# A gated projection from rounded parts and rests, and 20 of 31 depthwise taps as stacked diagonals in four column groups

## The reference, cut to what matters

```python
def conformer_conv_mixer(x, w_in, b_in, dw_w, dw_b, ln_g, ln_b, w_out, b_out):
    a = x @ w_in + b_in
    u = a[..., :D_MODEL] * jax.nn.sigmoid(a[..., D_MODEL:])
    u = causal_dwconv(u, dw_w, dw_b)
    u = jax.nn.silu(layernorm(u, ln_g, ln_b))
    return u @ w_out + b_out
```

## Time and profile before

| | us |
|---|---|
| three runs | 3436.68, 3441.87, 3441.95 (median 3441.87) |
| the profiled execution, first to last instruction (span) | 3435.1 |
| PE busy | 3336.9 (97%) |
| DVE busy | 2003.6 (58%) |
| ACT busy | 1111.1 (32%) |
| POOL busy | 134.1 (4%) |
| mean granted clock of PE | 0.989 |

### The profile page before, as it was taken

How to read it: one execution, slowest core, us unless ns; L and a number is a source line. 1 busy time by engine, 2 the same in 40 slices (tenths; PEclk the granted TensorE clock), 3 DMA queues, 4 the chain that set the end, 5 groups by cost and what they waited for, 6 DMA issues and landing times. The chain is left out here.

```text
span 3435.1 us, 38647 instructions
## 1 busy us (share of the span) xinstructions
PE 3336.9 (97%) x13840; PEld 2509.0 (73%) x13840; DVE 2003.6 (58%) x2815; ACT 1111.1 (32%) x1503; POOL 134.1 (4%) x230
## 2 busy tenths in 40 slices
PE   6999899998999999999999999999999999999999
PEld 3446788886678888667888854588887757888887
DVE  6684666535668864565766359766644464455523
ACT  2223422223632222444433210343333343242222
POOL 1000000000000000000000040000000100000000
PEclk9999999999999999999999999999999999999999
DMA  7222355542125543212223311122233222222222
GB/s 287 80 70 80 131 181 192 176 133 74 49 86 199 192 147 104 68 44 80 94 95 95 96 58 56 51 86 98 96 95 129 79 74 74 98 92 86 97 98 86
DMA packets 100426, 361.20 MB, mean 105 GB/s; under 512 B 11152, under 2 KB 11168, under 8 KB 100064
## 3 DMA queue, kind: packets, MB, share of 16 engines
q1 hardware_dynamic: 79088, 280.34, 24.6%
q0 software_dynamic: 20080, 75.27, 6.6%
q10 hardware_dynamic: 1152, 4.19, 0.3%
HBM read 357.66 MB, written 2.10 MB: 105 GB/s over the span
## 5 line engine op out<-in xcount | busy, mean ns | idle before, releaser
L2393 DVE TENSOR_TENSOR weight_lo<-weight_ring,weight_hi 128x1024 fp32r<-128x1024 f32 (+1 forms) x458 | 552.9, 1208 | 899.2 <-ACT weight_hi L1654 893.3
L1654 ACT ACTIVATE weight_hi<-weight_ring 128x1024 fp32r<-128x1024 f32 (+1 forms) x458 | 478.7, 1046 | 1558.8 <-PE proj_banks L919 972.3
L919 PE MATMUL proj_banks<-h_lo,weight_hi 128*128 128x512 f32 x1672 | 650.5, 389 | 0.0
L919 PE MATMUL proj_banks<-h_hi,weight_hi 128*128 128x512 f32 x1312 | 510.5, 389 | 0.5 <-DVE weight_lo L2393 0.5
L919 PE MATMUL proj_banks<-h_hi,weight_lo 128*128 128x512 f32 x1312 | 510.4, 389 | 0.0
L919 PEld LDWEIGHTS proj_banks<-h_lo,weight_hi 128*128 128x128 f32 x1672 | 313.8, 188 | 64.9
L919 PEld LDWEIGHTS proj_banks<-h_hi,weight_hi 128*128 128x128 f32 x1312 | 246.3, 188 | 52.3 <-issue 0.8
L919 PEld LDWEIGHTS proj_banks<-h_hi,weight_lo 128*128 128x128 f32 x1312 | 246.3, 188 | 51.0
L919 PE MATMUL proj_banks<-mid_lo,weight_hi 128*128 128x512 f32 x704 | 273.9, 389 | 0.0
L919 PE MATMUL proj_banks<-mid_hi,weight_lo 128*128 128x512 f32 x704 | 273.9, 389 | 0.0
L919 PE MATMUL proj_banks<-mid_hi,weight_hi 128*128 128x512 f32 x704 | 273.9, 389 | 0.0
(11 more groups left out here) (426 smaller groups left out, 5200.2 us busy)
## 6 DMA issues: line engine op xcount, KB each, us to landing
weight_ring<-in_w_up SPq DMA_DIRECT2D x176, 512.0 KB, 3.3
ada_ring<-in_ada POOLq DMA_DIRECT2D x96, 512.0 KB, 3.8
weight_ring<-in_w_dn SPq DMA_DIRECT2D x64, 512.0 KB, 3.5
weight_ring<-in_w_br SPq DMA_DIRECT2D x32, 512.0 KB, 3.2
weight_ring<-in_w_upr SPq DMA_DIRECT2D x32, 512.0 KB, 3.2
weight_ring<-in_w_dnr SPq DMA_DIRECT2D x32, 512.0 KB, 3.2
weight_ring<-in_w_dn SPq DMA_DIRECT2D x32, 384.0 KB, 3.1
cond<-in_ada POOLq DMA_DIRECT2D x20, 512.0 KB, 4.6
```

The costliest lines, as they stand in the source:

```text
L919: last = mm(proj.banks[:, u % RING, :], stationary(home + n)[:, w], moving(k), start=k + m == 0, stop=k == kt - 1 and m == 2)
L1654: return nc.scalar.activation(out, in_, func, **kw)
L2393: return v.tensor_tensor(out, a, b, op)
```

## The change

The projection `ca` joins `SPLIT`: weights and normed activations are split into rounded parts and rests, `first_three` does its tiles 0 to 2 (the third tile's weights go to a free part of the scratch memory), the other 13 are done by `split_feature_tile`. ACT and DVE split two chunks for each channel tile, placed between their other work. SP's loads for `ca` are written out instead of looped.

DVE keeps 11 taps of each channel tile; PE does 20. For these, SP copies `u` inside the SBUF: for each of the four groups of 32 channels, four copies, each one token further along, go to the four groups of 32 partitions (`spread_rows`, 16 DMAs of 32 x 528 floats for each tile, with two buffers in turn). One matmul then has 128 rows, four taps of 32 channels, and 32 columns: a 128 x 32 matrix in which four 32 x 32 diagonals are stacked (`stacked`). Five such matmuls, each four tokens further, make the 20 taps of 32 channels, and the four channel groups write the four groups of 32 partitions of one bank (`depthwise`). GpSimd makes all 20 x 4 small diagonals of a tile by one product of 128 x 640. The taps of tile t stand after the `ca` tile 2t + 3; those of the last tile stand between the sums of the first four tiles and of the last four.

```diff
+TAP_GROUPS = 5
+OWN_TAPS = CONV - 4 * TAP_GROUPS
+SPREAD = S + 4 * (TAP_GROUPS - 1)
...
+    def spread_rows(t):
+
+        if t >= 2:
+            sp.wait_ge(*c.mix.filled(("dw", t - 2)))
+        sp.wait_ge(*proj.emptied(("ca", 2 * t)))
+        u = c.T(0, 9)[:, t * PAD:(t + 1) * PAD]
+        for q in range(4):
+            for shift in range(4):
+                sp.dma_start(spread_taps(c, t)[32 * shift:32 * shift + 32, q, :],
+                             u[32 * q:32 * q + 32, OWN_TAPS + shift:OWN_TAPS + shift + SPREAD]).then_inc(s[f"taps_spread{t % 2}"], 16)
...
             load(name, n, first + n)
+            if name == "ca" and n >= 5 and n % 2 == 1:
+                spread_rows((n - 5) // 2)
+            if name == "cout" and n % 2 == 1:
+                spread_rows(6 + n // 2)
...
+    taps = 4 * TAP_GROUPS
     for t in range(KD):
-        for n, k in enumerate(range(CONV - PE_TAPS[t], CONV)):
-            nc.gpsimd.tensor_scalar(diagonal(c, t, n), c.square("ident"), c.v("c_dw_w_2", 8 * k + t), None, ALU.mult) \
-                .then_inc(s["diag_ready"], 1)
+        out = c.T(30, 10)[:, t * taps * 32:(t + 1) * taps * 32].rearrange("p (n i) -> p n i", i=32)
+        nc.gpsimd.tensor_tensor(out, c.const("eye32").unsqueeze(1).broadcast_to([P, taps, 32]),
+                                c.v("c_dw_stacked", t * taps, taps).unsqueeze(2).broadcast_to([P, taps, 32]), ALU.mult) \
+            .then_inc(s["diag_ready"], 1)
...
-    for t in range(KD + 1):
-        if t == 0:
-            feature_tile("ca", 0, H, ready=h_ready(6))
-            feature_tile("ca", 1, H)
-            continue
-        if t < KD:
-            feature_tile("ca", 2 * t, H)
-        if t == KD:
-            sum_squares(("lnm", 0), lambda k: (s["u_ready"], k + 1), lambda k: T(11 + k), KD, end=2)
-        pe.wait_ge(*proj.emptied(("ca", 2 * t - 2)))
-        pe.wait_ge(s["diag_ready"], TAPS_BEFORE[t])
-        u = T(0, 9)[:, (t - 1) * PAD:t * PAD]
-        bank = open_bank(mix, ("dw", t - 1))
-        for n, k in enumerate(range(CONV - PE_TAPS[t - 1], CONV)):
-            last = mm(bank, diagonal(c, t - 1, n), u[:, k:k + S], start=n == 0, stop=k == CONV - 1)
+    def depthwise(t):
+
+        pe.wait_ge(s["diag_ready"], t + 1)
+        pe.wait_ge(s[f"taps_spread{t % 2}"], 256 * (t // 2 + 1))
+        bank, x = open_bank(mix, ("dw", t)), spread_taps(c, t)
+        for g in range(TAP_GROUPS):
+            for q in range(4):
+                last = mm(bank[32 * q:32 * q + 32, :], stacked(c, t, g, q), x[:, q, 4 * g:4 * g + S], start=g == 0, stop=g == TAP_GROUPS - 1,
+                          skip_group_check=True)
         last.then_inc(mix.full_sem, 1)
-        if t < KD:
-            feature_tile("ca", 2 * t + 1, H)
-    sum_squares(("lnm", 0), lambda k: (s["u_ready"], k + 1), lambda k: T(11 + k), KD, first=2)
+
+    u_tile = lambda k: T(11 + k)
+    u_ready = lambda k: (s["u_ready"], k + 1)
+    first_three("ca", 6, c.H_lo)
+    for t in range(3, 16):
+        split_feature_tile("ca", t, c.H_hi, c.H_lo)
+        if t % 2 == 1:
+            depthwise((t - 3) // 2)
+    sum_squares(("lnm", 0), u_ready, u_tile, KD, end=4)
+    depthwise(7)
+    sum_squares(("lnm", 0), u_ready, u_tile, KD, first=4)
...
         copy_out(proj, ("ca", 2 * t + 1), T(9 + t % 2), ACT.Sigmoid, bias=c.v("c_b_in_2", 8 + t))
+        for n in range(2 * t + 3, min(2 * t + 5, 16)):
+            round_chunk("ca", n)
...
+    def add_spread(t):
+
+        dve.wait_ge(*mix.filled(("dw", t)))
+        st.last(tt(T(11 + t), T(11 + t), mix.bank(("dw", t)), ALU.add), mix.emptied(("dw", t)))
+        dve.sem_inc(s["u_ready"], 1)
+
     for t in range(KD):
-        u = u_all[:, t * pad:(t + 1) * pad]
-        if t < KD - 1:
-            gated(t)
-        acc, own = T(11 + t), CONV - PE_TAPS[t]
+        u, acc = u_all[:, t * pad:(t + 1) * pad], T(11 + t)
+        gated(t)
+        if 2 * t + 3 < 16:
+            rest_chunk("ca", 2 * t + 3)
         st.link(ts(acc, u[:, 0:S], c.v("c_dw_w_2", t), ALU.mult, c.v("c_dw_b_2", t), ALU.add))
...
+        for k in range(1, OWN_TAPS):
             st.link(stt(acc, u[:, k:k + S], c.v("c_dw_w_2", 8 * k + t), acc, ALU.mult, ALU.add))
...
+        if t >= 1:
+            add_spread(t - 1)
+        if 2 * t + 4 < 16:
+            rest_chunk("ca", 2 * t + 4)
+    add_spread(7)
```

More of the change, by code:

```diff
@@ L107, in other_constants @@
         "pick_wide": np.tile(np.eye(4, 32).reshape(1, 128), (P, 1)),
+        "eye32": np.tile(np.eye(32), (4, 1)),
     }
@@ L143 @@
     ("norm_mix_2", 2 * D), ("norm_ffn_2", 2 * D), ("norm_final_2", D), ("m_conv_w_2", 4 * D), ("m_conv_b_2", D),
-    ("m_head_norm_2", D), ("c_b_in_2", 2 * D), ("c_dw_w_2", CONV * D), ("c_dw_b_2", D), ("c_ln_g_2", D),
+    ("m_head_norm_2", D), ("c_b_in_2", 2 * D), ("c_dw_w_2", OWN_TAPS * D), ("c_dw_stacked", 4 * TAP_GROUPS * D), ("c_dw_b_2", D), ("c_ln_g_2", D),
     ("c_ln_b_2", D), ("c_b_out_2", D), ("f_conv_w_2", 2 * 3 * 2 * FF), ("f_conv_b_2", 2 * 2 * FF),
@@ L171 @@
 STAGE = {s[0]: s for s in STAGES}
-SPLIT = ("abo", "up0", "dn0", "sq", "sk", "sv", "cu", "cdo", "up1", "dn1", "mqk", "mv", "mo", "mout", "up2", "dn2", "cout", "up3", "dn3", "rk", "rq", "rv", "fv", "ru", "rg", "br", "ro", "upr", "dnr")
-SPLIT_NORMS = (1, 2, 3, 4, 5, 7, 9)
+SPLIT = ("abo", "up0", "dn0", "sq", "sk", "sv", "cu", "cdo", "up1", "dn1", "mqk", "mv", "mo", "mout", "up2", "dn2", "ca", "cout", "up3", "dn3", "rk", "rq", "rv", "fv", "ru", "rg", "br", "ro", "upr", "dnr")
+SPLIT_NORMS = (1, 2, 3, 4, 5, 6, 7, 9)
 def pieces(k_tiles):
@@ L389, in __init__ @@
             "gla_hi", "gla_lo", "dsa_hi", "pool_hi", "sb_hi", "m_hi", "m_lo_ready", "u_hi", "u_lo", "merged_hi", "merged_lo", "pooled", "z_ready", "k_scaled", "sp_ready", "lw_ready", "w_ready", "wneg_ready",
-            "diag_ready", "convolved", "conv_init", "conv_act", "mid_raw", "mid_rounded", "mid_ready", "w_rounded", "w_split", "third_rounded", "third_split", "w_used", "h_raw", "h_rounded", "m_gate", "m_rows", "m_guard", "e_arg", "e_ready",
+            "diag_ready", "taps_spread0", "taps_spread1", "convolved", "conv_init", "conv_act", "mid_raw", "mid_rounded", "mid_ready", "w_rounded", "w_split", "third_rounded", "third_split", "w_used", "h_raw", "h_rounded", "m_gate", "m_rows", "m_guard", "e_arg", "e_ready",
             "p_head", "hm_ready", "hsq_ready", "den_abs", "u_ready", "u_centred", "u_sq", "u_normed", "u_act",
@@ L596, in hi @@
             at = self.third[n][0]
-            return self.mid_hi[:, at * S:(at + 2) * S]
+            return (self.relu_r if n == self.first_split["ca"] + 2 else self.mid_hi)[:, at * S:(at + 2) * S]
         return self.w_hi[:, (n % SPLIT_RING) * SLOT:(n % SPLIT_RING + 1) * SLOT]
@@ L603, in lo @@
             at = self.third[n][1]
-            return self.mid_lo[:, at * S:(at + 2) * S]
+            return (self.relu_r if n == self.first_split["ca"] + 2 else self.mid_lo)[:, at * S:(at + 2) * S]
         return self.w_lo[:, (n % SPLIT_RING) * SLOT:(n % SPLIT_RING + 1) * SLOT]
@@ L667 @@
 PLAIN = {4: ("norm_mix_2", 0), 5: ("norm_ffn_2", 0), 6: ("norm_mix_2", 8), 7: ("norm_ffn_2", 8)}
-PLAIN_SPLIT = (4, 5, 7)
+PLAIN_SPLIT = (4, 5, 6, 7)
 SQ0, RSTD = 44, 54
@@ L714, in sync_program @@
             continue
-        looped = kind in ("loop", "branch")
+        looped = kind in ("loop", "branch") and name != "ca"
         for n in range(RING if looped else total):
@@ L1686, in round_third @@
         name = SPLIT_UP[r]
-        if NORM_AFTER[r] in ("dn0", "dn1"):
+        if NORM_AFTER[r] in ("dn0", "dn1", "dn2"):
             act.wait_ge(*split_use(c, c.first_split[NORM_AFTER[r]] + 3 * (KD - 1)))
@@ L2331, in scalar_program @@
         root_token("dnr", t, c.late_tile(4 + t))
-THIRD = {1: (16, 20), 2: (0, 2), 3: (16, 20), 4: (6, 0), 5: (14, 20), 7: (20, 20)}
-SPLIT_UP = {1: "up0", 2: "sq", 3: "up1", 4: "mqk", 5: "up2", 7: "up3"}
+THIRD = {1: (16, 20), 2: (0, 2), 3: (16, 20), 4: (6, 0), 5: (14, 20), 6: (24, 26), 7: (20, 20)}
+SPLIT_UP = {1: "up0", 2: "sq", 3: "up1", 4: "mqk", 5: "up2", 6: "ca", 7: "up3"}
 R_CHUNKS = [(name, n) for name in ("rk", "rq", "rv", "fv", "ru", "rg") for n in range(splits_of(STAGE[name]))] + [("br", 0), ("br", 1)]
@@ L2364, in split_use, with stacked, spread_taps @@
     return c.sem["w_used"], earlier + (per - 1) * (n // per) + n % per + 1
-PE_TAPS = [7] * (KD - 1) + [17]
-TAPS_BEFORE = [sum(PE_TAPS[:t]) for t in range(KD + 1)]
 PAD = S + CONV - 1
-def diagonal(c, t, n):
-    at = (TAPS_BEFORE[t] + n) * P
-    return c.T(19, 17)[:, at:at + P]
+def stacked(c, t, g, q):
+    at = ((t * TAP_GROUPS + g) * 4 + q) * 32
+    return c.T(30, 10)[:, at:at + 32]
+def spread_taps(c, t):
+    at = 19 * S + (t % 2) * 4 * SPREAD
+    return c.pool[:, at:at + 4 * SPREAD].rearrange("p (q w) -> p q w", q=4)
 EH = (53, 44)
@@ L3061, in vector_program @@
     st.link(v.memset(u_all.rearrange("p (k t) -> p k t", k=KD)[:, :, 0:CONV - 1], 0.0))
+    def add_spread(t):
+        dve.wait_ge(*mix.filled(("dw", t)))
```

(19 more changed lines are left out.)

## The result

The changed kernel takes 3474.27 us (median of 4, 3469.13 to 3477.95), the kernel before 3441.91 in the same comparison: ratio 1.0102 [1.0089, 1.0115]. It is 32 us **slower**, where 32.5 us less had been forecast.

A forecast was written before the change was run, and what follows sets the result against it. PE and DVE were both taken as full, PE busy 97% of the span. Cheaper projection and taps, less waits and clock loss, end the stage at 2146.7 instead of 2179.23: 3441.9 - 32.5 = 3409 us, range 3398 to 3428.

The forecast's parts named there:

- Behind that point all is as before: After DVE takes the layer-norm mean, forecast at 2146.7 in place of 2179.23, nothing changes, so the 32.5 us gain stays.
- The constants grow by 16 KB at the start: Constant load at kernel start: the added constants cost only 0.1 us of a load's 3.2.
- Projection: PE, `ca` matmuls: 109.8 us removed, 384 rounded matmuls at 0.2266 add 87.0, so 22.8 us saved.
- Taps: PE, stacked taps: all four column groups run at once, 4.5 us a tile, 36 in all, replacing 56.6.
- one at a time: Rival, PE's taps: column groups run singly, 17.4 us a tile, 99 us lost, 3508 us; chance 0.06.
- pairs: Rival, PE's taps: column groups overlap two by two, 8.8 us a tile, 30 lost, 3439 us; chance 0.03.
- partial overlap: Rival, PE's taps: groups overlap in part, 6.4 us a tile, 13.6 lost, 3423 us; chance 0.08.
- Pace: Steady stretch: PE alone sets the pace, two `ca` tiles and taps in 15.4 us; DVE needs 12.4.
- Copies: SP's 16 shifted copies a tile: issued 0.46 us apart, all landed 10.1 us after the gate, hidden except at first and last tile.
- The sum: Stage timeline: PE idles 1.2, 3.0 and 4.0 us, clock loses 1.4 together; mean taken at 2146.7, 32.5 us less.
- The low end of the range: Whole kernel: 3398 us, said to come from quick issue 5.6 us and clock 1.4 us better than 3409.
- GpSimd: Eight diagonal products of 640 columns take 2.96 us each, at most 5.9, hidden; rival that they hold up DVE: 3415, chance 0.03.

The follow-up runs named there:

- e1: Kernel before the change with only 32 unused columns (128 bytes a partition) added to the small constants, moving every tensor allocated behind them; 3493.89 us beside 3436.63.
- e9: Changed kernel with its 32-column identity in a tensor of its own behind all others, timed against the kernel before; 3415.91 us, ratio 0.9936.
- e7: Kernel before with a 128-byte gap behind the small tensors, so only the activations and scratch move; 3489.48 us.
- e11: Kernel before with a gap of 16 columns (64 bytes) between the small tensors and the big ones; 3477.60 us.
- e12: Kernel before with a gap of 8 columns (32 bytes) between the small tensors and the big ones; 3508.39 us.

## Why the prediction was wrong

**The step that failed** is "Behind that point all is as before", with the silent half of it, that all is as before ahead of the stage too. It rests on "The constants grow by 16 KB at the start, a 32nd of a 512 KB load: 0.1 us of its 3.2", which priced the transfer of the new constant and not its *place*. It measured some 58 us by the records (10,900 steps of 5.3 ns more in the mean; 57 us in e1, where nothing else changed). All rivals lay inside the stage, so none could hold it. An account of every tensor that moves, and not only of every instruction, would have shown the 128 bytes.

**Inside the stage**, step by step, with the tensors back in place (e9):
- Projection: one matmul every 0.2266, pair of tiles 10.9 us. Right; the 22.8 us are there.
- Taps: forecast 4.5 us a tile with 0.2 for going in and out of the small shape; measured 3.91 of starts and 0.43, 4.34, and 0.3 for going in and out. The four groups of a row start 7 ns apart (2108.986, .992, .999, 2109.006 in the changed kernel). The rivals one at a time, pairs and partial overlap fall. The Trainium skill ("TensorE: Matmul & The Clock Gate", Measured speedup vs the span model) gives 2.38 times for three column groups; here four gave 17.16 / 4.34 = 3.95.
- Pace: 15.4 forecast, 15.54 measured. DVE waits for PE, as said: for the sigmoids that ACT makes of PE's tiles. In the changed kernel, DVE's timeline shows it twice:

```profile
2157.30 0.75 DVE L2430 SCALAR_TENSOR_TENSOR scratch<-proj_banks,vectors,scratch 128x512 f32<-128x512 f32 x1 [3.01 <-ACT scratch L1677]
...
2168.05 0.69 DVE L2422 TENSOR_TENSOR scratch<-scratch,mix_banks 128x512 f32<-128x512 f32 x1
2173.06 0.75 DVE L2430 SCALAR_TENSOR_TENSOR scratch<-proj_banks,vectors,scratch 128x512 f32<-128x512 f32 x1 [4.33 <-ACT scratch L1677]
```

- Copies: SP's issues came 0.63 us apart, not the 0.46 of the earlier trace rows: 10.1 us for 16, as the end of the text feared ("over 8 us"). In the steady stretch PE's work still hides them.
- The sum: PE idles 1.01, 4.27 and 5.13 us at the three places where 1.2, 3.0 and 4.0 were forecast. The clock took 2.4 and 2.5 us, where 1.4 together was taken from the earlier trace rows. The first taps start 1.4 later from the start of the stage, six pairs lose 0.8, the second wait 1.1: 1.4 + 0.8 + 1.1 + 4.9 - 1.4 is 6.8 of the 6.9 us between 32.5 and the stage's 25.6. The mean is taken at 2154.34 where 2146 was forecast. (The low end of the range, 3398, does not follow from its terms: 5.6 and 1.4 below 3409 are 3402.)
- GpSimd: eight products in 11.97 us, where the forecast counted 2.96 for each. In the changed kernel they met DVE's rests once with a price (timeline of DVE; 1.23 is usual):

```profile
2038.60 1.62 DVE L2422 TENSOR_TENSOR weight_lo<-weight_ring,weight_hi 128x1024 fp32r<-128x1024 f32 x1
```

So the mechanism of the change was right and the gain it summed somewhat high; the sign was wrong for a cause outside it.

## What to carry to other kernels

A new constant has a place as well as a size: before and after an edit compare the memory map, and keep the moving tensors and the weights of long chains of rounded 512-column matmuls at the same place within 256 bytes (pad, or allocate the newcomer last): no other distance tried here was as fast. If untouched stages change their pace after an edit, count records in equal windows far from it before looking for a cause inside it. A wait for a chain of small transfers costs twice on PE, by the idle time and by the clock behind it; here other work filled it better than dummy matmuls, but see what the moved work will wait for.

## What the hardware showed that was not expected

- Rounded 128x512 matmuls in a row: 226.7 ns apart where both operands begin at the same byte modulo 256, up to 233.4 elsewhere. 256-column ones (`late_rounded` with weights in `relu_lo`) went the other way, 119.9 ns before and 118.7 in the changed kernel.
- The Trainium skill ("SBUF — State Buffer", Who interferes with whom) calls TensorE's two read ports, one for the moving operand and one for weights, independent. In e1, e7, e11 and e12 the pace hangs on how these two lie to each other; the measurement decides. Whether it is the ports or what lies behind them no run here shows.
- Two GpSimd products of 640 columns took 2.26 us and the others 1.29; the long ones began while DVE was at its rests, one of which took 1.62 us and the other 1.25.
